# A hybrid state-space and attention step on one core: gate blocks moved between the state-space products, output blocks between the next group's convolution blocks

## What is computed

```
zxbcdt = rmsnorm(h) @ w_in                       # z: 2048, x/B/C: 3072, dt: 32 columns
xbc    = silu(causal_conv(xbc, conv_buf, w, b))  # width 4
# per chunk: decay = exp(cumsum(dt * A)); four groups of 8 heads, state size 128
y   = (C B^T * decay) @ x*dt  +  (C @ S) * exp(acs)      # within the chunk, from the old state
S   = S * exp(acs_end) + B^T @ (x*dt * exp(acs_end - acs))
y   = rmsnorm((y + D*x) * silu(z)) @ w_out       # norm over all 2048 channels
h  += y
```

## Time and profile before

| | |
|---|---|
| median of three runs | 2033.18 us (2026.92 to 2036.0) |
| profiled execution, its own time | 2035.35 us |
| its span, first to last instruction | 2033.6 us |
| PE busy | 1916.4 us (94%) |
| DVE busy | 1150.3 us (57%) |
| ACT busy | 806.0 us (40%) |
| POOL busy | 338.6 us (17%) |
| mean granted PE clock | 0.963 |
| chain that ended last | PE 85%, DVE 8%, ACT 4% |

### The profile page before, as it was taken

One profiled execution on the slowest core, in us unless ns is written; L12 is line 12 of the kernel. 1 busy time (PEld: TensorE's weight loads), 2 busy tenths in 40 slices (PEclk: granted clock), 3 DMA queues, 4 the chain that ended last, 5 costly groups with the idle time before them and its releaser, 6 DMA issues.

```text
span 2033.6 us, 28519 instructions
## 1 busy us (share of the span) xinstructions
PE 1916.4 (94%) x10601; PEld 1778.3 (87%) x10601; DVE 1150.3 (57%) x1767; ACT 806.0 (40%) x1394; POOL 338.6 (17%) x423
## 2 busy tenths in 40 slices
PE   7999998899998699999999999988999999999997
PEld 6999998687786599999999999975666779999997
DVE  6555447667676855544685544465664555555444
ACT  4333326443534243333453333255444334333333
POOL 4000112414242500001310001231002213000011
PEclk9999998797998699999999999999999999999999
DMA  5444453445352244444444444441012213444441
GB/s 187 126 124 124 135 164 109 149 155 178 92 195 81 87 136 127 124 134 131 128 127 130 127 130 137 141 146 45 32 56 71 81 43 119 127 124 124 137 142 64
DMA packets 63413, 243.34 MB, mean 120 GB/s; under 512 B 7680, under 2 KB 7760, under 8 KB 62048
## 3 DMA queue, kind: packets, MB, share of 16 engines
q1 hardware_dynamic: 54000, 196.67, 31.2%
q0 software_dynamic: 9328, 45.51, 6.7%
HBM read 230.32 MB, written 11.83 MB: 119 GB/s over the span
## 4 chain that ended last, share of the span: by engine, by line
PE 85%; DVE 8%; ACT 4%; issue 2%; POOL 0%; DMA 0%; SPq 0%; DVEq 0%; ACTq 0%; POOLq 0%
PE bank L1472 23%; PE bank L1473 23%; PE bank L1474 23%; PE bank L1913 2%; PE bank L1870 1%; PE bank L1815 1%; PE bank L1622 1%; DVE wlo L976 1%; ACT seg L746 1%; PE bank L1626 1%; PE bank L1817 1%; ACT kn L886 1%; DVE xl L986 1%; PE bank L1816 1%; PE bank L1479 1%
## 5 line engine op out<-in xcount | busy, mean ns | idle before, releaser
L1472 PE MATMUL bank<-xh,whi 128*128 128x384 f32 x1928 | 657.7, 341 | 41.8 <-DVE xl L986 27.5
L1473 PE MATMUL bank<-xl,whi 128*128 128x384 f32 x1928 | 651.6, 338 | 0.0
L1474 PE MATMUL bank<-xh,wlo 128*128 128x384 f32 x1928 | 651.4, 338 | 0.0
L976 DVE TENSOR_TENSOR wlo<-raw,whi 128x1024 fp32r<-128x1024 f32 (+3 forms) x372 | 468.2, 1260 | 171.0 <-ACT whi L616 162.8
L616 ACT ACTIVATE whi<-raw 128x1024 fp32r<-128x1024 f32 (+2 forms) x369 | 379.2, 1029 | 283.7 <-PE bank L1474 271.8
L1472 PEld LDWEIGHTS bank<-xh,whi 128*128 128x128 f32 x1928 | 367.3, 191 | 55.2 <-issue 29.9
L1473 PEld LDWEIGHTS bank<-xl,whi 128*128 128x128 f32 x1928 | 368.0, 191 | 0.6
L1474 PEld LDWEIGHTS bank<-xh,wlo 128*128 128x128 f32 x1928 | 367.5, 191 | 0.0
L1472 PE MATMUL bank<-ah,whi 128*128 128x384 f32 x704 | 237.0, 337 | 3.5 <-DVE tu L997 3.3
L1473 PE MATMUL bank<-al,whi 128*128 128x384 f32 x704 | 236.5, 336 | 0.0
L1474 PE MATMUL bank<-ah,wlo 128*128 128x384 f32 x704 | 236.5, 336 | 0.0
(11 more groups left out here) (364 smaller groups left out, 2389.2 us busy)
## 6 DMA issues: line engine op xcount, KB each, us to landing
raw<-in_stream SPq DMA_DIRECT2D x372, 512.0 KB, 3.6
S<-in_ssm POOLq DMA_DIRECT2D x4, 2048.0 KB, 8.6
out_ssm_s<-S POOLq DMA_DIRECT2D x4, 2048.0 KB, 8.2
cTb<-in_cacheT POOLq DMA_DIRECT2D x16, 512.0 KB, 3.8
seg<-acs_rows POOLq DMA_DIRECT2D x12, 512.0 KB, 11.3
lowC<-in_cache POOLq DMA_DIRECT2D x8, 512.0 KB, 3.7
h<-in_x SPq DMA_DIRECT2D x2, 768.0 KB, 6.1
lowA<-in_wkT POOLq DMA_DIRECT2D x4, 384.0 KB, 5.5
```

The lines of the kernel that those rows point to most:

```text
L976: V.tensor_tensor(wlo[:, r, 0:w], raw[:, r, 0:w], whi[:, r, 0:w].bitcast(F32), ALU.subtract).then_inc(lo_ready, 1)
L1472: M(out, whi[:, r, ws], mh_(k), start=first and k == k0, stop=False)
L1473: M(out, whi[:, r, ws], ml_(k), start=False, stop=False)
L1474: ins = M(out, wlo[:, r, ws], mh_(k), start=False, stop=last and k == k1 - 1)
```

## The change

The list of blocks is put in a new order, and PE, DVE, ACT and the host's packing all read it. The gate blocks 7, 8 and 9 now stand between the state-space steps of their own group, and output blocks of group g between the input blocks of group g+1. The last group is different: two output blocks of group 2 wait until after its y tiles, and its y is kept in `xh`/`xl` rather than `yh`/`yl`. The same numbers of blocks, matmuls and split operations remain.

Banks: input blocks alternate between 6 and 7 (two of them use 1 and 2), output tiles between 4 and 5 except in the last group, sample states come in four pairs instead of two fours (banks 4 and 5, then 0 and 3). On ACT the eight Relu of a tile go between the next group's convolution blocks, and the three Exp follow in a row. On POOL the convolution of the next group goes ahead of the load of the states and of the squares. In the last group ACT squares y and DVE adds the squares.

```diff
+def mix_order():
+    order = [("in", 0, b) for b in range(10)]
+    for g in range(1, GROUPS):
+        last = g == GROUPS - 1
+        order += [("in", g, 0), ("in", g, 1), ("out", g - 1, 0), ("in", g, 2), ("out", g - 1, 1), ("in", g, 3), ("in", g, 4)]
+        order += [] if last else [("out", g - 1, 2)]
+        order += [("in", g, 5)]
+        order += [] if last else [("out", g - 1, 3)]
+        order += [("in", g, b) for b in range(6, 10)]
+    return order + [("out", GROUPS - 2, 2), ("out", GROUPS - 2, 3)] + [("out", GROUPS - 1, b) for b in range(4)]
-        LEAD = 2
+        IN_BANK = (6, 7, 1, 2, 6, 7, 6, 7, 6, 7)
+        def f_bank(g, j):
+            return bank[4 + (j % 4 if g == GROUPS - 1 or (g == GROUPS - 2 and j >= 4) else j % 2)]
```

PE, the waits of an input block and of an output block, and the order of a group:

```diff
                 if b >= 4:
-                    pe.wait_ge(in_evac, 10 * g + b - 3)
+                    pe.wait_ge(in_evac, 10 * g + b - 3 if b < 6 else 10 * g + b - 1)
+                elif g and b >= 2:
+                    pe.wait_ge(y_evac, 4 * (g - 1) + b)
                 elif g:
-                    pe.wait_ge(y_evac, 4 * (g - 1) + b + 1)
-                product(bank[b % 4][:, 0:TOK], n % SLOTS, 0, KD, *X, True, True).then_inc(blk, 1)
+                    pe.wait_ge(in_evac, 10 * g - 1 + b)
+                product(bank[IN_BANK[b]][:, 0:TOK], n % SLOTS, 0, KD, *X, True, True).then_inc(blk, 1)
...
+                    if b == 0 and g < GROUPS - 1:
+                        pe.wait_ge(state_ready, 8 * g + 6)
+                    elif g == GROUPS - 2 and b >= 2:
+                        pe.wait_ge(f_evac, 8 * g + 4)
+                        pe.wait_ge(state_ready, 8 * (g + 1) + 2 * b - 2)
+                    else:
+                        pe.wait_ge(f_evac, 8 * g + j - (3 if g == GROUPS - 1 else 1))
...
+            for g in range(GROUPS):
+                last = g == GROUPS - 1
+                in_proj(g, 0)
+                if g:
+                    sample_states(g - 1, 2)
+                in_proj(g, 1)
+                if g:
+                    sample_states(g - 1, 3)
+                    out_proj(g - 1, 0)
+                in_proj(g, 2)
+                if g:
+                    out_proj(g - 1, 1)
+                in_proj(g, 3)
+                in_proj(g, 4)
...
+                in_proj(g, 6)
+                if g == 0:
+                    decay_sums()
+                turns(g)
+                in_proj(g, 7)
+                first_states(g)
+                in_proj(g, 8)
+                old_state(g)
+                if g:
+                    y_tile(g, 0)
+                in_proj(g, 9)
+                if g == 0:
+                    y_tile(g, 0)
+                y_tile(g, 1)
+                sample_states(g, 0)
+                y_tile(g, 2)
+                sample_states(g, 1)
+            out_proj(GROUPS - 2, 2)
+            out_proj(GROUPS - 2, 3)
+            pe.wait_ge(y_evac, 4 * GROUPS)
+            pe.wait_ge(y_sq, 4 * GROUPS + 1)
+            M(bank[1][:, 0:TOK], ones[:, :], sqacc[:, 0, :], start=True, stop=True).then_inc(y_sum_ps, 1)
+            sample_states(GROUPS - 1, 2)
+            out_proj(GROUPS - 1, 0)
```

`turns` holds the transposes and G. In group 0 it waits, ahead of block 7, for `conv_done`, `acs_ready` and `da_ready` (ACT's exponentials of the decays). `first_states` is L1637, L1644 and L1638 of before, `old_state` is L1648. DVE, the end of the last group:

```diff
+            out_proj(GROUPS - 2, 2)
+            for i in range(4):
+                dve.wait_ge(y_sq, 4 * GROUPS - 3 + i)
+                ins = V.tensor_tensor(sqacc[:, 0, :], sqacc[:, 0, :], xsT[:, i, :], ALU.add)
...
+            out_proj(GROUPS - 2, 3)
+            state_add(GROUPS - 1, 2)
+            out_proj(GROUPS - 1, 0)
+            dve.wait_ge(y_std, 1)
+            step(V.reciprocal(rstd[:, 0, :], std[:, :]))
+            for b in range(1, 4):
+                residual(2 * b - 2)
+                residual(2 * b - 1)
+                out_proj(GROUPS - 1, b)
+                if b == 1:
+                    state_add(GROUPS - 1, 3)
+            residual(6)
+            residual(7)
```

More of the change, by code:

```diff
@@ L459, in _, with conv @@
             pool.memset(Cm[:, :, :], 0.0).then_inc(filled, 1)
-            for g in range(GROUPS):
+            def conv(g):
                 pool.wait_ge(c0_ready, 6 * g + POOL_TILE + 1)
@@ new lines, in seg_diff, with seg_exps, z_gate @@
+            def seg_diff(g, t):
+                act.wait_ge(seg_ld[t], 16 * (g + 1))
+                for hh in range(HPG):
+                    v = seg[:, t, tiles(hh)]
+                    ins = A(v, v, ACT.Relu, bias=acs[:, t, HPG * g + hh:HPG * g + hh + 1], scale=-1.0)
+                step(ins)
+            def seg_exps(g):
+                for t in range(TT):
+                    A(seg[:, t, :], seg[:, t, :], ACT.Exp, scale=-1.0).then_inc(decay_ready, 1)
+            def z_gate(g, i):
+                act.wait_ge(in_evac, 10 * g + 7 + i)
+                A(zs[:, i, :], zs[:, i, :], ACT.Silu).then_inc(z_done, 1)
```

538 lines of the change are left out of this document (312 added, 226 removed).

## The result

The changed kernel takes 2020.64 us (median of four runs, 2019.97 to 2021.01), the kernel before 2031.99 (four runs, 2026.92 to 2036.0): the ratio is 0.994, 95% interval 0.9925 to 0.9956. It is faster by 11 us, where 30 were forecast. The two profiled spans differ by 15.5 us (2033.6 and 2018.1).

The account below looks back on a forecast made before the run. PE, busy 94% of the span, was taken as the bound, losing time to waits and its lower clock. Gains 0 + 12.4 + 12.9 + 4.7 = 30.0 us off 2035.35 gave 2005.3, less 2.2 for the median: 2003 us, range 1991 to 2020.

Parts of the forecast that it names:

- group 0: First group of the mixer: a 6.8 us wait ahead of its first y tile, net gain 0, bounds -3 and +3.
- group 1: Middle group: 77.5 us plus 2.5 for starting at the lower clock, 80.0, a gain of 12.4 us.
- group 2: Middle group: 77.5 us at 2.4 GHz throughout against 90.4 before, a gain of 12.9 us.
- group 3 and end: Last group to the last split of h: 78.1 + 55 = 133 us against 137.7 before, gain 4.7.
- the price of a pair: Two sample states on PE, priced at 0.6 us; two times four sample states at 2.3 us a group.
- then eight residual tiles ... the last tile is split at about 55: Mixer's end: DVE is the chain from the last y tile, through sums and residual tiles, about 55 us.
- 0.5 + 1.5 + 0.5: Middle group's waits: 0.5 us at the pair behind block 1, 1.5 for the first output tile's bank, 0.5 for small waits.
- After that DVE has blocks without convolution in between, and catches up: Output blocks of a middle group: after the 1.5 us wait for the first output tile's bank, DVE catches up.
- Rival (1): DVE falls behind in the groups, convolutions slow beside POOL: 5.5 us a group, 2019; 2028 with a full lock; chance 0.17.
- Rival (2): More comes back: ACT keeps up in group 3 and group 0's first decays come 2 to 3 us sooner, 1992; chance 0.12.
- Rival (3): PE's clock falls at the two bank hand-offs in a group: 13.9 us lost in each of groups 1 to 3, 2040; chance 0.04.
- Rival (4): The waits only move: groups 0 and 3 each lose 10 us more through a late ACT step, 2023; chance 0.05.

Follow-up runs that it names:

- states in fours: The "four together" kernel with groups 0 to 2's sample states made in two fours, not four pairs, and group 3's first four in one piece: 1995.3 us.
- gate blocks in a row: The changed kernel with gate blocks 8 and 9 again in a row behind block 7 in groups 1 to 3, output blocks still interleaved: 2047.15 us.
- ACT's order at the end: The changed kernel with ACT's rounding of h for tiles 0 to 3 placed between its last weight-block roundings at the mixer's end: 2017.2 us.
- Relu early in group 0 and in group 3: Two runs on the changed kernel: group 0's 24 Relu ahead of the rounding for block 9, 2009.5 us; group 3's ahead of convolution blocks 2 and 3, 2012.6 us.
- four together: The changed kernel with four output-tile banks, earlier Relu in group 0 and in groups 1 to 3, and ACT's new order at the mixer's end: 2002.19 us.
- sum on PE: The "four together" kernel with the last group's squares added up by PE as four further products, not by DVE's four additions: 1994.7 us.
- all: The "four together" kernel plus the edits of "states in fours", "order of group 0" and "sum on PE": 1984.51 us, ratio 0.975 to the kernel before.
- order of group 0: The "four together" kernel with group 0's block 7 ahead of the transposes, later gate blocks a step earlier, DVE's decay products before block 9's evacuation: 1996.6 us.

## Why the prediction was wrong

The forecast was 2003 us, 1991 to 2020; the kernel takes 2020.6. The mechanism was right: the waits for `seg` and for y's banks went in groups 1 and 2, the clock there went to 0.97 and 1.00. The periods, 81.45 and 80.44 us, are above the 76 to 80 that were named for it. The size was off by half: 15.5 us of 30 between the profiled spans. By its own marks (the end counted to the last split of `h`, 689.70 in the trace after):

| step | gain forecast | measured | |
|---|---|---|---|
| group 0 | 0 | -2.9 | 90.36 for 87.44 |
| group 1 | 12.4 | 11.0 | 81.45, forecast 80.0 |
| group 2 | 12.9 | 9.9 | 80.44, forecast 77.5 |
| group 3 and end | 4.7 | -0.5 | 77.59 + 60.58, forecast 78.1 + 55 |
| rest of the program | 0 | -2.0 | |
| spans | 30.0 | 15.5 | |

**First failing step: the price of a pair.** "PE does block 0, a state pair, block 1: 4.15 + 0.6 + 4.15", and "two times four sample states take 2.3". I halved the price of a four. A pair costs 1.06 us at full clock and 2.01 at half (380.21 to 382.22). Four pairs are 4.24 where 2.3 stood, 1.9 us in each of groups 1 to 3, and the two of group 0, at half clock, are 2.0 more: 7.8 us in all. The run with the states in fours got 2.3 of work a group back. The Trainium skill says it outright, in TensorE: Matmul & The Clock Gate, section Part 3: Packing small matmuls — row/col tiling: products whose operands sit in different 32-row strips of the array run side by side. The traces agree: eight matmuls in 1.14 us, four in 1.13. The count of instructions was right; what changed is how many stand together.

**Second failing step: "then eight residual tiles ... the last tile is split at about 55".** I followed DVE and POOL and did not ask where ACT's `x_hi` stands in its program: behind three weight roundings, the last of which waits for output block 2. DVE lost 5.52 us, PE 4.06 and its clock. The run with ACT's order altered returned 6.8 us.

These two are 13.4 us (7.8 and 60.58 - 55); the four steps fell short by 12.5. What is left nearly cancels. Blocks behind small products take 4.2 to 4.6 us where I had 4.15 (about 1.1 a group). The waits I had spread over the start of a group (0.5 + 1.5 + 0.5) came as one, 1.70 and 2.39, ahead of output block 3, not 1; in group 3, which carried the same 2.5, none of them came, and its 77.59 us are near the forecast's 78.1 by that luck. "After that DVE has blocks without convolution in between, and catches up" was thus wrong too, but it cost only what I had allowed. So was the "nothing" for POOL's convolution of block 2: ACT waits 1.05 us for it, on the chain to that wait. The other named waits were close: 5.82 for 6.8 ahead of the first y tile of group 0, 3.21 (1.19 and 2.02) for 3 ahead of its G, 5.92 for 6.4 ahead of group 3's transposes.

**From spans to medians** another 4 us of the gain went: the profiled execution of the kernel before lies 3.4 over its median, that of the changed one 0.7 under its own. I took 2.2 off both, so 2.9 of the 17.5 us between 2003 and 2020.6 come from there.

Rival (1), DVE behind, described the wait that came, but its size, 5.5 a group, was not there: 1.70 and 2.39 us of wait lie within the 2.5 that the forecast held. That DVE and POOL hold each other up is in the rows: the three operations of the convolution take 3.83 us beside the squares and 1.99 without, and POOL's eight decays took 10.73 us in group 1, where the earlier trace rows have 9.43. Three of DVE's operations beside those decays took 1.87, 1.88 and 0.93 us for 1.23, 1.22 and 0.68 alone, 1.6 us more in all, where the forecast had 3, and no wait of PE came of it. The Trainium skill calls it an exclusive lock (SBUF — State Buffer, SBUF: two separate sides). A lock for all of the decays' time, 3 us a group more, did not show; whether it is a lock or a sharing, these rows do not tell.

Rival (2), more comes back, did not happen: the waits of 5.82 us in group 0 and 5.92 in group 3 came nearly as forecast. Rival (3), the fallen clock, did not come in the changed kernel's profile: in groups 1 and 2 a wait of 1.70 or 2.39 us stood between full blocks, at a clock of 0.97 and 1.00. That was luck for group 2. Four other kernels have the same wait there, 2.38 or 2.39 us (gate blocks in a row, ACT's order at the end, and Relu early in group 0 and in group 3), and in all four the clock fell behind it. The changed kernel and "Relu early, group 0", in the 3 us behind the wait:

```profile
514.10:517.10 3.00, 3.00 (x17) 3.00 (x18) 2.96 (x6) 2.05 (x8) 0.00 (x0) 1.00 0.58 175
512.29:515.29 3.00, 3.00 (x9) 3.00 (x10) 2.96 (x6) 2.06 (x8) 0.00 (x0) 0.50 0.58 175
```

It cost 1.4 us, 81.8 for 80.44 in the three that have nothing else altered in group 2; the wait of 1.70 in group 1 had no such fall in any of the five. So such a fall behind a hand-off of banks does happen, at a tenth of the 13.9 us a group that the rival had for it. The Trainium skill (TensorE: Matmul & The Clock Gate, A second HAM failure mode: psum-queue depth-cycling) has a kernel that lost its clock again and again while it cycled its PSUM queue; behind these waits the traces show single falls, not a series.

Rival (4), waits that move into groups 0 and 3, is the nearest in its time (2023). Its "one late ACT step" did come, ACT's first `x_hi` at the end, for 5.6 us; the extra 2.9 us of group 0 did not come from a late step but mostly from the pairs.

## What to carry to other kernels

The price of a small product belongs to the group in which it is issued; before a group of products is split, ask whether they ran side by side. When a chain is costed, write down for every link where it stands in the program of the engine that makes it, not only when its inputs are ready. And test the parts of a reordering together: where each removes one of two waits of a loop, either one alone can be a loss.

## What the runs showed of the hardware

- Two and four fp32 products of 32 rows in different strips take the same time, 1.06 and 1.07 us to the next start.
- The clock after one and the same wait is not the same from run to run. With the same program in group 0 and a wait of 5.81 or 5.82 us ahead of its first y tile, PE ran at 1.2 GHz into the next block in the changed kernel (a pair of states took 2.08 us, group 0 90.36), and was back at 2.4 GHz within 4 us of its restart in "ACT's order at the end" (1.13, and 82.96). The wait of 2.39 us ahead of output block 3 in group 2 left the clock alone in one of five profiles and took it down for 3 to 4 us in four.
- In six kernels PE waited 2.91 or 2.92 us ahead of the first y tile of group 0. In the three with one program there ("Relu early, group 0", "four together", "sum on PE") it ran at 1.2 GHz from there into the next block, and group 0 takes 85 to 88 us; in "states in fours" and "all" it was back at 2.4 GHz within 6 us; in "order of group 0" it never left it, and these three take 75 to 79. Their programs of group 0 differ in small things, so this is no proof that the edits kept the clock up. What decides it these traces don't show.
- The rest of the program, from the next stage on the same instructions, took 1314.3 to 1323.8 us in the fourteen profiles, and in steps: 1314.3 in three, 1317.2 to 1317.5 in four, 1320.1 to 1321.1 in three, 1323.7 or 1323.8 in four. PE's busy time for its 7077 matmuls moves along (1269.7 us in one of the shortest, 1279.4 in one of the longest), so the steps are most likely the clock's. Medians of four or five runs could not rank alterations worth 2 or 3 us, and windows by stage could only where the clock had not moved inside the stage.
